# A two-block transformer kernel: the second attention's small projections, and the small loads, put in another order

## The reference, cut to what matters

```
u = rms_norm(h, norm_mix_pre)                     # 528 x 1024
proj = u @ w_in
dq, dk, dv, dz, db, da, aq, ak, av = split(proj)  # 512 x4, 8, 8, 512, 128, 128 wide
beta = sigmoid(db)
g = -exp(a_log) * softplus(da + dt_bias)          # the log decay
gc = cumsum(g) inside a chunk                     # both directions
o_dn = gated delta rule over dq, dk, dv with beta, gc, exp(gc), exp(g_last - gc); gated by dz
o_at = attention(rope(rms_norm(aq)), rope(rms_norm(ak)), av)   # 8 query heads, 2 kv heads
mix = concat(o_dn, o_at) @ w_out ;  h += rms_norm(mix)
u = rms_norm(h, norm_mlp_pre) ;  h += rms_norm(square(relu(u @ w_up)) @ w_down)
```

## Time and profile before

| | us |
|---|---|
| median of three runs | 1539.74 |
| lowest, highest | 1537.80, 1542.81 |
| the profiled execution | 1539.06 |
| its span, first to last instruction | 1537.2 |
| busy: PE, DVE, ACT, POOL | 1407.7, 728.0, 422.2, 789.6 |
| mean granted TensorE clock | 0.957 |

### The profile page before, as it was taken

One profiled execution on the slowest core, in us unless ns is written; L12 is line 12 of the kernel. 1 busy time (PEld: TensorE's weight loads), 2 busy tenths in 40 slices (PEclk: granted clock), 3 DMA queues, 4 the chain that ended last, 5 costly groups with the idle time before them and its releaser, 6 DMA issues.

```text
span 1537.2 us, 20352 instructions
## 1 busy us (share of the span) xinstructions
PE 1407.7 (92%) x7564; PEld 1153.4 (75%) x7564; DVE 728.0 (47%) x1080; ACT 422.2 (27%) x833; POOL 789.6 (51%) x459
## 2 busy tenths in 40 slices
PE   5889699988999999999798999876997999999996
PEld 3667477767888888888697888756875888888884
DVE  5778545554545556211555888377716111211112
ACT  3123334432221222110324445442424111111111
POOL 4556433435666666666061633223263766666661
PEclk9899899999999999999998999996998999999998
DMA  4222112112222222232130111100021322222221
GB/s 169 69 83 83 55 56 68 55 55 83 96 96 96 96 96 96 96 96 82 43 110 28 42 56 56 42 1 2 1 83 45 118 96 96 96 96 96 96 82 55
DMA packets 31740, 113.87 MB, mean 74 GB/s; under 512 B 3520, under 2 KB 3904, under 8 KB 31424
## 3 DMA queue, kind: packets, MB, share of 16 engines
q1 hardware_dynamic: 31680, 113.03, 22.2%
HBM read 110.92 MB, written 2.10 MB: 74 GB/s over the span
## 4 chain that ended last, share of the span: by engine, by line
PE 82%; DVE 12%; ACT 3%; issue 2%; DMA 1%; POOL 0%; SPq 0%; DVEq 0%; POOLq 0%; ACTq 0%
PE ps L993 39%; PE ps L1183 18%; PE ps L1326 6%; ACT arena L535 3%; PE ps L1012 2%; PE ps L1033 2%; PE ps L1026 2%; DVE arena L1651 2%; PE ps L1203 1%; PE ps L1300 1%; PE ps L1135 1%; PE ps L1280 1%; DVE arena L1603 1%; PE ps L1124 1%; DVE arena L1946 1%
## 5 line engine op out<-in xcount | busy, mean ns | idle before, releaser
L454 POOL TENSOR_SCALAR w_hi<-raw 128x1024 fp32r<-128x1024 f32 x204 | 222.9, 1093 | 626.7 <-PE ps L993 221.1
L456 POOL TENSOR_TENSOR w_lo<-raw,w_hi 128x1024 fp32r<-128x1024 f32 x204 | 516.7, 2533 | 17.1
L993 PE MATMUL ps<-h_hi,w_hi 128*128 128x512 f32 (+1 forms) x976 | 378.2, 393 | 17.1 <-ACT arena L535 10.0
L993 PE MATMUL ps<-h_lo,w_hi 128*128 128x512 f32 (+1 forms) x976 | 371.8, 386 | 0.0
L993 PE MATMUL ps<-h_hi,w_lo 128*128 128x512 f32 (+1 forms) x976 | 371.4, 386 | 0.0
L993 PEld LDWEIGHTS ps<-h_hi,w_hi 128*128 128x128 f32 x976 | 184.0, 191 | 62.9 <-issue 16.2
L993 PEld LDWEIGHTS ps<-h_lo,w_hi 128*128 128x128 f32 x976 | 183.8, 191 | 37.5 <-issue 2.2
L993 PEld LDWEIGHTS ps<-h_hi,w_lo 128*128 128x128 f32 x976 | 183.4, 190 | 36.2
L535 ACT ACTIVATE arena<-ps 128x512 f32<-128x512 f32 (+7 forms) x213 | 101.1, 508 | 301.2 <-PE ps L993 125.1
L535 ACT ACTIVATE arena<-arena 128x512 f32<-128x512 f32 (+6 forms) x190 | 101.3, 536 | 231.3 <-DVE arena L2191 134.3
L1183 PE MATMUL ps<-g_hi,w_hi 128*128 128x512 f32 x400 | 155.9, 390 | 0.9 <-DVE arena L1819 0.9
(11 more groups left out here) (269 smaller groups left out, 1872.1 us busy)
## 6 DMA issues: line engine op xcount, KB each, us to landing
raw<-in_w_stream SPq DMA_DIRECT2D x204, 512.0 KB, 3.5
xT<-in_x_t SPq DMA_DIRECT2D x2, 1056.0 KB, 6.5
out<-xT SPq DMA_DIRECT2D x8, 256.0 KB, 2.1
C<-in_cst SPq DMA_DIRECT2D x1, 576.0 KB, 9.3
arena<-in_cst SPq DMA_DIRECT2D x1, 528.0 KB, 3.5
arena<-in_pos SPq DMA_DIRECT2D x1, 256.0 KB, 4.0
V<-in_vec SPq DMA_DIRECT2D x1, 174.5 KB, 7.9
band<-in_cst SPq DMA_DIRECT2D x1, 160.5 KB, 3.7
```

The lines of the kernel that those rows point to most:

```text
L454: pool.tensor_scalar(w_hi[j][:], raw[j % 2][:], 1.0, 1.0, ALU.mult, ALU.mult).then_inc(S["pool_step"], 1)
L456: pool.tensor_tensor(w_lo[j][:], raw[j % 2][:], w_hi[j][:], ALU.subtract).then_inc(split_done[j], 1)
L993: last = mm(dst[p], w[:, k, :], h[:, k, cols], start=(k == 0 and n == 0), stop=(k == KT - 1 and n == 2))
```

## The change

It has four parts. (1) On SP the wait, the table of angles and the small weights move from behind round 28 to behind round 13 of the loads (after unit 51), and the wait is for `x_ready` 1; the later units then follow one another without a further wait. The small weights and the two small-projection buffers get other places in the arena. (2) Masks and the split of the small weights move on DVE and ACT ahead of the norm's root and parts. (3) PE does the small projection right behind units 110 and 111, into banks 4 and 5, then the transposes of V, `k2_side(0)` and the transposes of the small projection into bank 2; unit 113 waits for `bat_ready` 2. `k2_side(4)` and `scores2(0)` go into unit 116, and the ten sums ahead of it. (4) On ACT and DVE the decay's steps are cut into four pieces and put behind the query tiles 0, 1, 2 and 4, the last two steps (`tables`) behind the first `norm2`.

```diff
+        bat = n_h[0:16, 0, :]
+        bac = n_h[:, 1, 0:80].rearrange("p (a b) -> p a b", b=16)
+        wba32 = arena[:, AC - 6 * L - P:AC - 6 * L].rearrange("p (a b) -> p a b", b=16)
 # SP
-            N_FIRST = -(-U_AT2 // 4)
+            N_FIRST = U_UP // 4 + 2
             rep(sp, N_FIRST, load)
-            sp.wait_ge(S["h_ready"], 32)
+            sp.wait_ge(S["x_ready"], 1)
             sp.dma_start(arena[:, p4 + 2 * L + 640:p4 + 4 * L + 640], cst2).then_inc(S["c2_loaded"], 16)
             sp.dma_start(wba32, w_ba).then_inc(S["ba_loaded"], 16)
 # ACT
-            root(2, ...)
-            high(3, slice(0, L))
             act.wait_ge(S["ba_loaded"], 16)
             act.wait_ge(S["ba_split"], 1)
             a(wba_hi[:, :, 0:16], wba32, ACT.Copy).then_inc(S["ba_split"], 1)
+            root(2, ...)
+            high(3, slice(0, L))
...
             a(flat(x5[:, 1, 0:L]), two(1), ACT.Copy).then_inc(S["t2_read"], 1)
+            act.wait_ge(S["ba_rows"], 1)
+            a(bat.rearrange("p (a b) -> p a b", a=2), ps[0:16, 4:6, 0:HALF], ACT.Copy).then_inc(S["bat_ready"], 1)
+            (the wait for v2_turned and the two avtok copies, from behind kb2_ready)
             k2_root(0)
+            act.wait_ge(S["ba_done"], 1)
+            a(bac, ps[:, 2, 0:80].rearrange("p (a b) -> p a b", b=16), ACT.Copy).then_inc(S["bat_ready"], 1)
             k2_in(1, 2, U_AT2 + 2, vcol("q_norm2"))
...
             for t in range(1, 4):
                 k2_in(t + 1, t + 2, U_AT2 + 2 + t, vcol("q_norm2"))
                 k2_root(t)
+                if t == 1:
+                    act.wait_ge(S["bat_ready"], 2)
+                    act.wait_ge(S["ba_ready"], 1)
+                    a(tb[0], bac[:, :, 0:8], ACT.Tanh, scale=0.5)
+                    log_set()
+                    a(tb[2], tb[2], ACT.Exp, scale=-1.0)
+                    a(small2[:, 8:16], V[:, VOFF["a_log"]:VOFF["a_log"] + 8], ACT.Exp).then_inc(S["tab_ready"], 1)
+                if t == 2:
+                    act.wait_ge(S["ba_ready"], 2)
+                    a(NBE, tb[3], ACT.Ln).then_inc(S["tab_ready"], 1)
             k2_root(4)
...
             def dn_copy(d):
                 product(act, U_DN2 + d)
+                if d == 0:
+                    act.wait_ge(S["k2_dve"], 5)
 # PE
             def wide(n, u):
+                if n == 3:
+                    pe.wait_ge(S["bat_ready"], 2)
             def k2_side(t):
+                if t == 0:
+                    pe.wait_ge(S["bat_ready"], 1)
...
             tile_pair(U_AT2, 3, [two(0), two(1)], halves)
+            pe.wait_ge(S["ba_split"], 3)
+            (the 48 matmuls of the small projection into ps[:, 4 + c]; ba_rows)
+            pe.wait_ge(S["t2_read"], 2)
+            (the five transposes of V; v2_turned)
             k2_side(0)
+            (the five transposes of bat into ps[:, 2]; ba_done)
             wide(2, U_AT2 + 2)
             (swap product; kb2_done)
             for t in range(1, 4):
                 wide(2 + t, U_AT2 + 2 + t)
                 k2_side(t)
-            (small projection, k2_side(4), waits for k2_dve 5 and bat_ready 1, transposes of bat)
...
 # wide_part
-                    pe.wait_ge(S["t2_read"], 6 + d)
+                    pe.wait_ge(S["t2_read"], 6 + d if d else 5)
...
-            wide_part(0, range(0, 4))
-            scores2(0)
-            wide_part(0, range(4, 8))
             pe.wait_ge(S["ba_ready"], 3)
+            pe.wait_ge(S["v2_ready"], 1)
             (the ten sums of the log decay; gc_done)
+            wide_part(0, range(0, 3))
+            k2_side(4)
+            wide_part(0, range(3, 5))
+            pe.wait_ge(S["k2_dve"], 4)
+            pe.wait_ge(S["k2_sqrt"], 5)
+            pe.wait_ge(S["t2_read"], 6)
+            scores2(0)
+            wide_part(0, range(5, 8))
+            pe.wait_ge(S["k2_dve"], 5)
             pe.wait_ge(S["ba_ready"], 4)
             pe.wait_ge(S["tab_ready"], 3)
 # DVE
-            dve.wait_ge(S["rs_ready"], 3)
-            parts(3, slice(0, L), gained("mix_pre", slice(0, L)))
             (masks, wba_hi and wba_lo cleared, wba_lo split: ba_split 1 and 3)
+            dve.wait_ge(S["rs_ready"], 3)
+            parts(3, slice(0, L), gained("mix_pre", slice(0, L)))
...
             for t in range(5):
                 (rotation of tile t; k2_dve)
+                if t == 0:
+                    gate_input()      # waits bat_ready 2; 3 steps; ba_ready 1
+                if t == 1:
+                    one_plus()        # waits tab_ready 1; 7 steps; ba_ready 2
+                if t == 2:
+                    log_decay()       # waits tab_ready 2; 3 steps: G (ba_ready 3), BETA
+            sums_read()               # waits gc_done; 2 steps; ba_ready 4
             v.memset(x5[:, :, 0:2], 0.0)
             v.memset(x5[:, :, L + 2:L + 4], 0.0).then_inc(S["pads_ready"], 1)
...
             for n in range(2):
                 norm2(n)
+            tables()                  # waits tab_ready 3; 2 steps
```

More of the change, by code:

```diff
@@ L1238, in _ @@
             tile_pair(U_AT2, 3, [two(0), two(1)], halves)
+            pe.wait_ge(S["ba_split"], 3)
+            for k in range(KT):
+                for n, (w, h) in enumerate(((wba_hi, h_hi), (wba_hi, h_lo), (wba_lo, h_hi))):
+                    for c in range(2):
+                        last = mm(ps[:, 4 + c, 0:HALF], w[:, k, :], h[:, k, halves[c]], start=(k == 0 and n == 0), stop=(k == KT - 1 and n == 2))
+            last.then_inc(S["ba_rows"], 1)
+            pe.wait_ge(S["t2_read"], 2)
+            for b in range(5):
+                c0 = META + P * b if b < 4 else 0
+                last = nc.tensor.transpose(ps[:, 6 + b // 4, (b % 4) * P:(b % 4) * P + P], x5[:, 1, c0:c0 + P], cst_ap("ident"))
+            last.then_inc(S["v2_turned"], 1)
             k2_side(0)
+            for b in range(5):
+                c0 = META + P * b if b < 4 else 0
+                last = nc.tensor.transpose(ps[:, 2, 16 * b:16 * b + 16], bat[:, c0:c0 + P], cst_ap("ident")[0:16, 0:16])
+            last.then_inc(S["ba_done"], 1)
             wide(2, U_AT2 + 2)
@@ L1245, in _ @@
             last.then_inc(S["kb2_done"], 1)
[L1246 to L1250, removed]
             for t in range(1, 4):
@@ L1253, in _ @@
                 k2_side(t)
[L1256 to L1270, removed]
             def scores2(q):
@@ L1860, in _, with row, gate_input @@
             v.tensor_tensor(wba_lo[:, :, 0:16], wba32, wba_hi[:, :, 0:16], ALU.subtract).then_inc(S["ba_split"], 1)
+            dve.wait_ge(S["rs_ready"], 3)
+            parts(3, slice(0, L), gained("mix_pre", slice(0, L)))
             def flat(x):
                 return x.rearrange("p (a b) -> p a b", a=2)
+            def row(name):
+                return V[:, VOFF[name]:VOFF[name] + 8].unsqueeze(1).to_broadcast([P, 5, 8])
+            def gate_input():
+                dve.wait_ge(S["bat_ready"], 2)
+                step(v.tensor_tensor(tb[1], bac[:, :, 8:16], row("dt_bias"), ALU.add))
+                step.settle()
+                step(v.tensor_scalar(tb[2], tb[1], -1.0, None, ALU.mult))
+                step.settle()
+                v.tensor_tensor(tb[2], tb[2], tb[1], ALU.max).then_inc(S["ba_ready"], 1)
@@ new lines, in one_plus @@
+            def one_plus():
+                dve.wait_ge(S["tab_ready"], 1)
+                v.tensor_scalar(tb[3], tb[2], 1.0, None, ALU.add).then_inc(S["ba_ready"], 1)
+                dve.wait_ge(S["ba_ready"], 2)
+                step(v.tensor_scalar(GCC, tb[3], 1.0, None, ALU.subtract))
+                step.settle()
+                step(v.tensor_tensor(GCC, tb[2], GCC, ALU.subtract))
+                step.settle()
+                step(v.reciprocal(tb[2], tb[3]))
+                step(v.tensor_scalar(tb[1], tb[1], 0.0, None, ALU.max))
+                step.settle()
+                step(v.tensor_tensor(GCC, GCC, tb[2], ALU.mult))
+                step.settle()
+                step(v.tensor_tensor(GCC, GCC, tb[1], ALU.add))
+                step.settle()
@@ new lines, in log_decay @@
+            def log_decay():
+                dve.wait_ge(S["tab_ready"], 2)
+                step(v.tensor_tensor(GCC, GCC, NBE, ALU.add))
+                step.settle()
+                v.scalar_tensor_tensor(out=G, in0=GCC, scalar=-1.0, in1=small2[:, 8:16].unsqueeze(1).to_broadcast([P, 5, 8]),
+                                       op0=ALU.mult, op1=ALU.mult).then_inc(S["ba_ready"], 1)
+                step(v.tensor_scalar(BETA, tb[0], 0.5, 0.5, ALU.mult, ALU.add))
+                step.settle()
@@ new lines, in sums_read, with tables @@
+            def sums_read():
+                dve.wait_ge(S["gc_done"], 1)
+                step(v.tensor_copy(GCC, ps[:, 6, 0:40].rearrange("p (a b) -> p a b", b=8)))
+                step.settle()
+                v.tensor_tensor(KD, ps[:, 6, 40:80].rearrange("p (a b) -> p a b", b=8), GCC, ALU.subtract).then_inc(S["ba_ready"], 1)
+            def tables():
+                dve.wait_ge(S["tab_ready"], 3)
```

(12 more changed lines are left out.)

51 lines of the change are left out of this document (5 added, 46 removed).

## The result

The changed kernel takes 1524.81 us (median of five runs, 1522.86 to 1526.31). The kernel before, run beside it on the same chip, takes 1537.8 (five runs, 1535.28 to 1542.81). The ratio is 0.9904, 95% interval 0.9889 to 0.9919. The profiled executions have spans of 1524.0 and 1537.2 us: 13.2 us less. Forecast were 1524.4 us and a gain of 14.7.

What follows compares the result with a forecast made beforehand. TensorE, with 82% of the chain of waits, was taken as the bound, with three gaps and clock tails to shorten. 44.1 + 3.1 + 0.9 = 48.1 us against 62.8 gains 14.7: 1539.06 - 14.7 = 1524.4 us, range 1519.5 to 1531.

Steps and rivals of the forecast that it cites:

- TensorE's order: TensorE's moved work from the end of units 110 and 111 to the end of unit 116: 44.1 us.
- The end of it: From unit 116's end to the loop's first transposes: 3.1 us, plus 0.9 for normalising beside a split (bounds 0 and 1.5).
- VectorE's queue: Query tiles and decay steps on VectorE: G ready at 797, wanted at 798.2, slack 1.2 us; cost 0 (bounds 0 and 1.8).
- the yardstick's time: Clock of the profile before, whose yardstick runs from units 110 and 111's end (763.2) to the loop's first transposes (826.04).
- Rival 1: ScalarE's table switches at tile 1 hold VectorE, so TensorE waits at the sums: 2 to 5 us lost; chance 0.13.
- The table loads: ScalarE's two switches after tile 1's root: 1.28 us each; with the skill's 1.38 us drain each, a 1.6 us stall.
- Masks and small split: Five VectorE steps (1.7 us) and a ScalarE copy moved ahead of the norm, ending by 745.5: cost 0, bounds 0 and 1.
- SP's queue and the early loads: Loads moved to the first MLP's up stage: cost 0, or 3.5 us without cover; no gain counted for them alone.
- Clock: The new 4 us gap before the loop has a half-clock tail like the old 3.2 us one: cancels; bounds 1.6 either way.
- Rival 3: Light work between 763 and 807 leaves TensorE at half clock from unit 112 to 116: 29 us lost, 1553; chance 0.04.
- The sum: From the end of units 110 and 111 to the loop's first transposes: 48.1 us against 62.8, a gain of 14.7.

Runs made afterwards that it cites:

- Experiment 5: Changed kernel with GpSimd's split of unit 120 held until after the second normalising step: 1523.72 us, ratio 0.9904 to the kernel before.
- Experiment 4: Changed kernel with beta made from Exp instead of Tanh, dropping two table loads at tile 1: 1522.91 us, ratio 0.9879 to the kernel before.
- experiment 6: Changed kernel with the pair of table loads at tile 1 doubled, 3 us of delay: 1534.88 us, ratio 0.9971 to the kernel before.
- experiment 1: Changed kernel with loads, masks and small-weight split back in their old places, new order kept: 1527.36 us, ratio 0.9906 to the kernel before.
- experiment 2: Kernel before with only the early loads, masks and small split, old projection order: 1533.78 us, ratio 0.9957; repeated once, 1528.01 us.
- experiment 8: Version 7 with the splits of units 118, 119 and 120 held until the probabilities are there: 1526.58 us, ratio 0.9919 to the kernel before.
- experiment 3: Changed kernel with the first two softmax exponentials ahead of ScalarE's copies of unit 116's product: 1523.07 us, ratio 0.9887 to the kernel before.
- Version 7: Changed kernel without tile 1's table switch, exponentials ahead of the copies, unit 120's split after normalising: 1520.67 us, ratio 0.9888 to the kernel before.
- experiment 9: Kernel of experiment 8 plus four unused matmuls on constants in the gap ahead of the norm: 1524.8 us, ratio 0.9904 to the kernel before.

## Why the prediction was right, and where its sizes were off

**TensorE's order.** Right. The sum had unit 116 ending 44.1 us after unit 111, it ended at 44.9. Of the 0.8 us of difference, 0.2 had come up by the ten sums (unit 112 took 6.07 instead of 5.85, the wait for ScalarE's copy at 769.70 was 0.23 instead of 0.1), and 0.6 between there and the end of unit 116, whose pieces cost more at their joints than the forecast's 5.9 had in them (0.07 of it idle ahead of `scores2(0)`). No wait of TensorE exceeds 0.3 us up to unit 116.

**The end of it.** Right, and the contention came out inside its bounds of 0 and 1.5: the normalising step took 1.52 us instead of 0.49 beside the split that began at 808.87, so 1.03 where I took 0.9. The rest, from the end of unit 116 to the first transposes, took 3.0, forecast 3.1. VectorE's timeline of the changed kernel:

```profile
811.11 1.52 DVE L1956 TENSOR_SCALAR arena<-arena 128x528 f32<-128x528 f32 x1
...
812.74 0.49 DVE L1956 TENSOR_SCALAR arena<-arena 128x528 f32<-128x528 f32 x1
```

Experiment 5 takes the 1.03 away alone, so it is shown.

**VectorE's queue.** In the yardstick's time, 0.6 us ahead of the changed kernel's clock, G was to stand at 797 and be wanted at 798.2. It stood at 798.37 (797.8) and was wanted at 799.06: slack 0.7 us, not 1.2. This was the tied queue of the chain. Tile 2 was beside the split of 118 as said (2.31 us for a step), and tile 3 beside that of 119, which I had not counted (2.79). At the sums the slack that was left covered this. At the end it did not: tile 4, forecast for 806, ended at 807.5, and the two steps behind it, which ScalarE's exponentials wait for, at 807.8, later than the 807.3 at which unit 116 was to end. It came out at no cost because unit 116 itself was 0.8 late, which is luck. Experiment 4 shows that less delay gives nothing, experiment 6 that more delay costs more than twice itself. Rival 1 was thus rightly placed, but undersized: 2 to 5 us for it, where 3 us of delay made 7.2.

**The table loads.** ScalarE's timeline of the changed kernel:

```profile
786.65 0.65 ACT L537 ACTIVATE arena<-arena 128x528 f32<-128x528 f32 x1
787.31 1.28 ACT L537 ACT_TABLE_LOAD   x1
788.61 0.24 ACT L537 ACTIVATE arena<-arena 128x40 f32<-128x40 f32 x1
788.85 1.28 ACT L551 ACT_TABLE_LOAD   x1
```

Each load starts within 0.01 us behind the step ahead of it and the next step 0.01 to 0.02 behind the load. The Trainium skill ("ScalarE: Activation LUTs", What ACT_TABLE_LOAD costs) adds some 1.38 us of drain to each; these rows show none, and the stall of 1.6 us at the sums that the prediction worked out from it did not come.

**Masks and small split.** Cost nothing, as taken, but with the cover nearly gone. VectorE's timeline of the changed kernel, then GpSimd's:

```profile
739.07 3.53 DVE L1855 CAST masks<-C 128x128 fp32r<-128x128 f32 x3
742.52 2.86 DVE L1858 TENSOR_SCALAR g_hi<-C 128x1024 fp32r<-128x1024 f32 x1
...
746.41 0.29 DVE L1862 TENSOR_TENSOR g_lo<-arena,g_hi 128x128 fp32r<-128x128 f32 x1 [0.44 <-ACT g_hi L537]
...
748.05 1.45 DVE L1609 SCALAR_TENSOR_TENSOR arena<-xT,V,arena 128x528 f32<-128x528 f32 x2 [1.34 <-ACT arena L537]
```

```profile
737.90 1.04 POOL L456 TENSOR_SCALAR w_hi<-raw 128x1024 fp32r<-128x1024 f32 x1 [6.65 <-PE ps L1207]
...
742.47 2.36 POOL L458 TENSOR_TENSOR w_lo<-raw,w_hi 128x1024 fp32r<-128x1024 f32 x1
```

Beside the splits of units 112 and 113 the VectorE steps took 7.2 us where I had 1.7 alone, and ended at 746.7 (746.1 in the yardstick's time) against my 745.5. The norm's first step still started 0.58 later than before, just the shift of the whole execution, because ScalarE's root released it. ScalarE had 0.26 us to spare ahead of that root. The size was off, the bound of 0 to 1 held.

**SP's queue and the early loads.** The move cost 0, the loads landed 4.5 us after their issue (3.5 before) and nobody waited. "I count nothing for them alone" was 0.6 short at this place: experiment 1 has 49.6 against 48.98, for the split weights came 0.35 us after TensorE wanted them and the projection took 0.29 us longer. The prediction's reason holds, the same gap is filled twice.

**Clock.** Right: the new tail is 3.5 us at 0.54; the first transposes and 24 matmuls together took 5.22 us against 1.30 + 3.95 before. Rival 3 is refuted: 27.2 us from 772.0 at 1.00, with all the side products and sums in them.

**The sum.** 48.98 against 48.1 is 0.9 of the missing 1.5 us; the other 0.6 is the constant shift from the up stage. By medians the gain is 13.0 us, 1.7 less than forecast. That the median, 1524.81, still lies 0.4 us from the forecast of 1524.4 is partly luck: the runs of the kernel before that stood beside it had a median 1.9 us lower than the one the forecast started near. And the 62.8 us are read from one execution; experiment 2 shows that the clock behind such a gap, and with it a gap's price, differs between executions of one kernel.

## What to carry to other kernels

Fill a stall with independent work that already exists, and price each part by the gap that it fills, not by the stall that it removes: two edits for one gap give it once. When TensorE looks full, follow the chain to see whether another queue is tied with it; here such a queue gave nothing back when it was relieved and took more than its delay when it was pushed. Work of GpSimd that is moved out of VectorE's way can land beside other VectorE steps, as in experiment 8: ask first which ones. Price a clock tail from more than one execution.

## What the runs showed of the hardware that I had not expected

- **Small VectorE steps lose most beside a GpSimd split**, in proportion: steps of 40 columns take 0.18 to 0.20 us alone, 0.92 and 1.64 beside one; the three casts of 128 columns took 3.53 us in all, 0.49 alone before. The held steps end with the split's part that they lie beside, 0.04 to 0.6 us behind it, so a step that starts earlier is not done earlier (experiments 3 and 4).
- **The clock behind a wait is not fixed by its length.** TensorE's 2.26 us ahead of the transposes of beta and decay were followed by 6.3 us at 0.50 in the kernel before, and by 6.4 us at 0.73 in one execution of experiment 2's kernel and at 1.00 in the other. The 2.21 us at the start of the delta-rule stage were followed by 1.00 in eight of the fourteen profiled executions, and by 0.50 to 0.67 over the next 4 us in six. Version 7's 2.0 us had no tail, the changed kernel's 4.1 us had 3.5 us at 0.54, and the 4.2 us of experiment 6 had 6.5 us at 0.52. The gap ahead of the norm, of 3.8 us, has 0.87 over the pair, and 1.00 when matmuls on constants fill it (experiment 9). What decides between the outcomes of one wait stays open.
